# Issuing the ada weight rows between the projection weights in one written-out order, in a two-block transformer kernel

## The reference

```
mod = silu(c) @ ada_w + ada_b                 # 1024 x 6144; split into sh1, sc1, g1, sh2, sc2, g2
h = rms_norm(x, norm1_g) * (1 + sc1) + sh1
proj = h @ w_in + b_in                        # 2304 columns: q 512, k 128, v 128, gb 512, gc 512, xs 512
q, k = rope(q), rope(k)                       # 8 query heads, 2 key heads of 64
y_attn = sliding_window_attention(q, k, v, sinks)
y_conv = gc * causal_dwconv3(gb * xs, conv_w)
x = x + g1 * (concat(rms_norm(y_attn), rms_norm(y_conv)) @ w_o)
...                                           # gated FFN with sh2, sc2, g2; then a second block
```

## Time and profile before

| | |
|---|---|
| median of 3 runs | 2206.54 us (2206.42 to 2210.15) |
| profiled execution | 2206.54 us, of which the profile's span is 2204.8 us |
| TensorE busy | 92% of the span |
| VectorE, ScalarE, GpSimd busy | 49%, 36%, 10% |
| mean granted TensorE clock | 0.95 of full |
| first block's mixer (to the FFN's first matmul) | about 0 to 290 us |

### The profile page before, as it was taken

The page is one execution under the profiler, slowest core; times in us unless marked ns, Lnnn a source line. Parts: engine busy times, 40 slices in busy tenths (PEclk is TensorE's granted clock), DMA queues, the critical chain, the costliest instruction groups (busy, mean ns, idle before and its releaser), DMA issues.

```text
span 2204.8 us, 35366 instructions
## 1 busy us (share of the span) xinstructions
PE 2026.2 (92%) x14391; PEld 1583.1 (72%) x14391; DVE 1078.8 (49%) x1571; ACT 785.1 (36%) x1243; POOL 213.8 (10%) x231
## 2 busy tenths in 40 slices
PE   7998989999996988799989899999989779999997
PEld 5776768888871666577767688888768557888885
DVE  6777765544227343677642644432253544444323
ACT  4334233333222333566633322332243433332221
POOL 0000000000013000222211011110000011111100
PEclk8999989999998999699989999999989889999998
DMA  8544223333321222000002133343223022333330
GB/s 290 162 134 125 86 61 92 95 95 109 104 71 34 67 77 68 7 9 8 7 25 68 56 95 97 99 115 92 64 72 99 12 75 86 95 95 99 110 87 39
DMA packets 311051, 181.00 MB, mean 82 GB/s; under 512 B 16381, under 2 KB 303763, under 8 KB 310932
## 3 DMA queue, kind: packets, MB, share of 16 engines
q1 hardware_dynamic: 310114, 179.07, 27.5%
q10 hardware_dynamic: 818, 0.21, 0.0%
HBM read 177.16 MB, written 2.10 MB: 81 GB/s over the span
## 4 chain that ended last, share of the span: by engine, by line
PE 85%; DVE 8%; ACT 3%; issue 2%; ACTq 0%; POOL 0%; DVEq 0%; POOLq 0%
PE bank L247 23%; PE bank L248 22%; PE bank L249 22%; PE bank L1898 4%; DVE rstd L351 2%; PE bank L441 1%; PE bank L333 1%; PE bank L2379 1%; PE bank L2373 1%; PE bank L2480 1%; ACT whi L226 1%; DVE tmp L1248 1%; DVE x L1253 0%; ACTq L617 0%; PE bank L1036 0%
## 5 line engine op out<-in xcount | busy, mean ns | idle before, releaser
L232 DVE TENSOR_TENSOR wlo<-raw,whi 128x1024 fp32r<-128x1024 f32 (+1 forms) x262 | 340.2, 1299 | 772.9 <-ACT whi L226 772.8
L226 ACT ACTIVATE whi<-raw 128x1024 fp32r<-128x1024 f32 (+1 forms) x262 | 293.1, 1119 | 777.5 <-PE bank L249 775.6
L247 PE MATMUL bank<-fh_hi,whi 128*128 128x512 f32 x1056 | 421.2, 399 | 26.7 <-DVE fh_lo L415 19.4
L248 PE MATMUL bank<-fh_lo,whi 128*128 128x512 f32 x1056 | 415.0, 393 | 0.0
L249 PE MATMUL bank<-fh_hi,wlo 128*128 128x512 f32 x1056 | 414.9, 393 | 0.0
L247 PEld LDWEIGHTS bank<-fh_hi,whi 128*128 128x128 f32 x1056 | 199.2, 189 | 84.4 <-DVE fh_lo L415 29.9
L248 PEld LDWEIGHTS bank<-fh_lo,whi 128*128 128x128 f32 x1056 | 199.4, 189 | 45.1 <-issue 2.4
L249 PEld LDWEIGHTS bank<-fh_hi,wlo 128*128 128x128 f32 x1056 | 199.2, 189 | 43.6
L248 PE MATMUL bank<-f_lo,whi 128*128 128x512 f32 x528 | 205.6, 389 | 0.0
L247 PE MATMUL bank<-f_hi,whi 128*128 128x512 f32 x528 | 205.6, 389 | 0.0
L249 PE MATMUL bank<-f_hi,wlo 128*128 128x512 f32 x528 | 205.6, 389 | 0.0
(11 more groups left out here) (398 smaller groups left out, 3125.2 us busy)
## 6 DMA issues: line engine op xcount, KB each, us to landing
raw<-in_w_up_dram SPq DMA_DIRECT2D x44, 512.0 KB, 3.8
raw<-in_ffn_w_gate_dram SPq DMA_DIRECT2D x44, 512.0 KB, 3.8
raw<-in_ffn_w_up_dram SPq DMA_DIRECT2D x44, 512.0 KB, 3.8
raw<-in_ffn_w_down_dram SPq DMA_DIRECT2D x32, 704.0 KB, 4.6
late<-in_ada_w_dram SPq DMA_DIRECT2D x32, 512.0 KB, 4.0
raw<-in_rwkv_w_rkv_dram SPq DMA_DIRECT2D x24, 512.0 KB, 4.0
raw<-in_w_down_dram SPq DMA_DIRECT2D x16, 704.0 KB, 4.6
early<-in_ada_w_dram SPq DMA_DIRECT2D x16, 512.0 KB, 14.8
```

The costliest lines, as they stand in the source:

```text
L226: act.activation(whi[:, at.slot, 0:kts * P], raw_unit(at, kts), ACT.Copy).then_inc(hi_ready, 1)
L232: dve.tensor_tensor(wlo[:, at.slot, 0:kts * P], raw_unit(at, kts), whi[:, at.slot, 0:kts * P].bitcast(F32), ALU.subtract).then_inc(lo_read ...
L247: pe.matmul(dst, hi, rhs_hi(k), start=first and k == 0, stop=False)
L248: pe.matmul(dst, hi, rhs_lo(k), start=False, stop=False)
```

## The change

The rule that built `order` is replaced. Before, a late block was put by the unit in which VectorE uses it: the first four behind unit 3, and block m+4 six entries behind the unit that uses m. Now each unit is followed by a fixed number of late blocks: two after the even and one after the odd units of 0 to 11, one after each of 12 to 17, and one after each `w_o` unit. The slots, the waits of each entry, the instructions of the other four engines and their order are as they were; the three ranges that VectorE reads are only defined further down.

```diff
-    AHEAD = 2 + RAW
-    used_in = {m: u for u in range(len(LATE_IN)) for m in LATE_IN[u]}
-    used_in.update({m: len(LATE_IN) - 1 + i * (N_IN - len(LATE_IN)) // len(LATE_STEP)
-                    for i, m in enumerate(LATE_STEP)})
-    units = [("in", u) for u in range(N_IN)] + [("o", u) for u in range(N_O)]
-    order = []
-    for n, unit in enumerate(units):
-        order.append(unit)
-        if n == RAW - 1:
-            order += [("late", m) for m in range(EARLY, EARLY + RAW)]
-        order += [("late", m + RAW) for m in used_in if used_in[m] + AHEAD == n and m + RAW < 6 * KD]
-    order += [("late", m) for m in range(EARLY, 6 * KD) if ("late", m) not in order]
+    order, m = [], EARLY
+    for u in range(N_IN):
+        order.append(("in", u))
+        for _ in range(2 - u % 2 if u < 12 else 1):
+            order.append(("late", m))
+            m += 1
+    for u in range(N_O):
+        order.append(("o", u))
+        if m < 6 * KD:
+            order.append(("late", m))
+            m += 1
```

More of the change, by code:

```diff
@@ L452, in build @@
     EARLY = 2 * KD
-    LATE_IN = [range(EARLY + a, EARLY + b) for a, b in ((0, 1), (1, 3), (3, 5), (5, 7), (7, 9), (9, 10))]
-    LATE_STEP = range(EARLY + 10, EARLY + 26)
-    LATE_OUT = range(EARLY + 26, 6 * KD)
-    AHEAD = 2 + RAW
-    used_in = {m: u for u in range(len(LATE_IN)) for m in LATE_IN[u]}
-    used_in.update({m: len(LATE_IN) - 1 + i * (N_IN - len(LATE_IN)) // len(LATE_STEP)
-                    for i, m in enumerate(LATE_STEP)})
-    units = [("in", u) for u in range(N_IN)] + [("o", u) for u in range(N_O)]
-    order = []
-    for n, unit in enumerate(units):
-        order.append(unit)
-        if n == RAW - 1:
-            order += [("late", m) for m in range(EARLY, EARLY + RAW)]
-        order += [("late", m + RAW) for m in used_in if used_in[m] + AHEAD == n and m + RAW < 6 * KD]
-    order += [("late", m) for m in range(EARLY, 6 * KD) if ("late", m) not in order]
+    order, m = [], EARLY
[9 more added lines that the diff above has]
+            m += 1
     at_in, at_o, seq = {}, {}, []
@@ L1210, in build @@
     o_used = sem("o_used")
+    LATE_IN = [range(EARLY + a, EARLY + b) for a, b in ((0, 1), (1, 3), (3, 5), (5, 7), (7, 9), (9, 10))]
+    LATE_STEP = range(EARLY + 10, EARLY + 26)
+    LATE_OUT = range(EARLY + 26, 6 * KD)
     OUT_BANKS = ((0, 1), (2, 3), (PV, PT))
```

## The result

The changed kernel takes 2223.06 us (median of 4 runs, 2221.89 to 2225.13) against 2206.48 us (median of 4, 2205.27 to 2210.15): ratio 1.0074, 95% interval 1.0056 to 1.0091. It is slower by 16.6 us. Its profiled execution took 2221.25 us, with a span of 2219.5 us, 14.7 over the one before.

The account below looks back on a forecast made before the run. Loads were early and TensorE busy throughout the q, k and v units; the new order makes loops of SP, DMA, ScalarE and VectorE. Scores 15.7 us late plus 0.9 for clock gives 16.6; 2206.5 + 16.6 = 2223, range 2214 to 2230.

Parts of the forecast that it names:

- Start: Blocks 16 and 17 ahead of unit 1 delay its rounding to 40.4 us; costs nothing, with 3 us to spare.
- First hop: Unit 3 waits in SP's queue behind block 20, released at 62.35 us, and lands at 68.3.
- Rounding to release: From ScalarE's rounding of a unit to VectorE's release of the next block: 1.16 us, then 4.38 us.
- Second and third hop: Units 4 and 5 behind blocks 21 and 23: closed loops of 11.1 us each, against TensorE's 6.35 per unit.
- Last hop: Unit 7 behind blocks 25 and 26: low part starts at 104.3 instead of 88.53 us, first scores 15.7 us late.
- Unit 6 costs nothing: Unit 6 needs block 20's use and comes close behind unit 5 in SP's queue, so it adds no delay.
- Clock: TensorE's longer pause before the first scores lowers its clock behind them: 0 to 1.7 us, taken as 0.9.
- The rest of the kernel: From the first scores to the end, no later unit is late; the traces stay 16 to 17 us apart.
- Hidden: Rival, chance 0.04: the q, k and v stage hides all delay, needing at most 6.35 us per round; 2206.5 us.
- one or two hops only: Rival, chance 0.08: a load runs ahead by one block, opening the loop; 5 or 10 us lost, 2211 to 2216.
- The clock joins in: Rival, chance 0.10: TensorE's idle time lowers its clock and loads take 6.2 us; 2229 to 2232 us.
- Faster: Rival, chance 0.03: the shift moves TensorE's low-clock stretches off the path, winning back over 21 us; about 2200 us.

Follow-up runs that it names:

- the series hop by hop: Changed kernel's order with unit 3, units 3 and 4, or units 3 to 5 put ahead of block 20: ratios 1.0038, 1.0034, 1.0005 to the kernel before.

## Why the prediction was right, point by point

**Start: nothing.** Unit 1's rounding moved from 36.35 to 39.07, less than the 40.4 expected, and TensorE stayed the one that VectorE waited for. Right.

**First hop.** Predicted from 62.35 to a rounding at 68.4; measured from 62.8 to 69.00, so 6.2 instead of 6.05 us, behind a start 0.4 us later in this run.

**Rounding to release.** 1.15 us (69.00 to 70.15) and 4.38 (to 74.53), as read from the rows before. Between rounding and release nothing changes when the load is late, since ScalarE and VectorE work through the same list. The wait for loads itself I had put at "some 20 us in all"; it is 41.6, of which 3.9 is unit 1. In a round of 11.1 us ScalarE works for 1.7 and waits for the rest, about 9.3 each time, also for the part that it had spent waiting for TensorE before. So the sign with which I wanted to see the delay was half of what the prediction's own rounds imply; the delay doesn't hang on it.

**Second and third hop.** 11.1 us each predicted; 11.06 and 10.94 between the roundings. The landings were 5.1 and 5.0 us.

**Last hop.** This term was mis-sized: 5.1 us predicted, 7.3 measured. I had used the landing behind one block, though two stand ahead of unit 7, and had moreover put the 6.2 of the slowest row into a rival only. My range allowed 1.1 to 1.3 us for each of three landings, where the chain has four, and this one alone was 2.2 off. Low part of unit 7: 15.75 us late predicted; measured 106.72 against 88.53, 18.2, of which 0.4 is the later start and 2.2 this landing. The scores were expected at 107 to 108 and came at 109.93.

**Unit 6 costs nothing.** Nearly: it waited for its load too (94.59), yet VectorE took it only at 97.81, behind blocks 21 and 22.

**Clock.** TensorE paused for 2.0, 4.5 and 1.9 us, as expected, and for 5.5 before the scores. I expected 0 to 1.7 us behind the scores. From the scores to the first matmul of the FFN the two traces are equally long: 91.74 to 290.49, 198.75 us, and 109.93 to 308.81, 198.88. So in this pair of traces the term is about 0.1. The pause is longer and its clock lower (0.62 against 1.00), but the stretch of work behind it has 0.73 in both. Over the q, k and v units the clock was 0.87, and no cost shows, as the hops say.

**The rest of the kernel.** "The two traces run in parallel, apart by 16 to 17 us" was not right for this pair of profiles: they are 18.3 us apart at the FFN, 15.3 where the second block's FFN begins, and 14.7 at the end. The same matmuls of the norm of that FFN in the trace before and after:

```profile
1226.65 1.02 PE L441 MATMUL bank<-sq,ones 128*128 128x512 f32 x2
```

```profile
1241.99 1.02 PE L441 MATMUL bank<-sq,ones 128*128 128x512 f32 x2
```

Between them lies the same work in 936.2 and 933.2 us, with a granted clock of 0.94 and 0.95. The difference arises between 880 and 1230 us, where the same 7072 matmuls take 350.0 and 347.0 us. The kernel with the new order only up to unit 7 has a span of 2222.7 us, 17.9 over the one before. The 29 executions of the kernel before beside the first experiments lie between 2198.12 and 2214.16 us. So I take the 3 us for scatter from execution to execution; that isn't shown, and why they fell in that stretch stays open. That the median hit 2223 to a tenth is partly luck: the prediction's 16.6 is a delay of 15.75 and 0.9 for the clock, and the trace has 17.8 and 0.1.

**The rivals.** "Hidden" and "one or two hops only" fell with the series hop by hop, and so did a single hop that carries all of it. "The clock joins in" had one part right, a landing above 5.1 us, and its price for the clock wrong. "Faster" would have needed 21 us of clock to come back; the span gave back 3. The estimate from the Trainium skill's page "DMA: Bandwidth & Descriptors", section "Anatomy of one DMA", 2215, would have been 8 us off: the landings of units 4, 5 and 7 in the changed kernel were 5.1, 5.0 and 7.3 us. The rule there is for loads issued by GpSimd; where GpSimd issues the blocks here, between SP's loads, the median landing is 4.2 us (20 to 300 us), not the 3.2 of the rule either.

## What to carry to other kernels

In a queue that issues in order, an entry with a wait lends this wait to all behind it. For each entry ask which instruction releases it, and whether that instruction itself comes behind something that the entries behind are to deliver: if so, prefetch has become a loop, and each round costs issue, landing and the consumers' work: here 11 us, with the DMA engines busy for 0.51 of the stretch instead of 0.81. One more slot, the entries one unit later, or another queue opens it, and each of these took away all of the loss.

## What the runs showed of the hardware that was not expected

The stretch before unit 2 has two lengths, with the same instructions. From 31.2 to 46.0 us, before and in the kernel with the old order up to unit 7 (windows, columns as in the earlier trace rows):

```profile
31.20:46.00 14.80, 14.68 (x80) 14.36 (x79) 9.56 (x7) 5.68 (x10) 0.00 (x0) 0.50 1.03 267
```

```profile
31.20:46.00 14.80, 12.17 (x78) 11.84 (x77) 11.90 (x11) 6.76 (x12) 0.00 (x0) 0.58 1.09 285
```

TensorE does here many small matmuls with one column, and is granted 1.2 of its 2.4 GHz for most of the stretch. In the one trace the first 2.2 us have a granted clock of 0.51; in the other they have 1.00, the mean of the whole is 0.58 instead of 0.50, and the rounding of unit 2 starts 2.4 us sooner. Of twelve profiles six show the one and six the other. The order of the queue does not decide it: the changed kernel and the two with unit 7 moved are the same up to unit 6, and the first starts late (59.68) and the two early (57.00, 56.79). What decides it is not shown. An offset of 2.4 us between two traces is therefore no sign of a change; a comparison is to be made from a common event behind it.

The landing of a unit of 512 KB doesn't follow from the loads just ahead of it alone. Behind one block, issued 0.4 us before, it took 4.9 to 5.1 us in the hops above, but 6.2 in the slowest row and 6.1 for unit 4 with the blocks one unit later. Behind two blocks, issued 1.8 and 0.4 us before, unit 7 took between 6.0 and 7.6 us in the five versions that have these two blocks just ahead of it (7.6 with the new order only up to unit 7). Within the changed kernel's order, taking one of the two blocks away took 7.3 down to 4.9. So the second block costs, but the size of the cost varies with something that no run here isolates.
